# Seven half-size products in place of eight, in the query and output projections of a memory attention on one Trainium2 core

## What is computed

```python
def memory_cross_attention(h, mem_n, wq, wk, wv, wo):
    b, s, _ = h.shape                       # 1, 512
    q = (h @ wq).reshape(b, s, 4, 256)      # wq, wk, wv, wo: 1024 x 1024
    k = (mem_n @ wk).reshape(b, m, 4, 256)  # m = 256
    v = (mem_n @ wv).reshape(b, m, 4, 256)
    logits = jnp.einsum('bqhd,bkhd->bhqk', q, k) * 256 ** -0.5
    probs = jax.nn.softmax(logits, axis=-1)
    out = jnp.einsum('bhqk,bkhd->bqhd', probs, v).reshape(b, s, 1024)
    return out @ wo

# in each of the two layers of the first block
x = x + hybrid_mixer(...)
x = x + memory_cross_attention(rms_norm(x, ...), rms_norm(mem, ...), wq, wk, wv, wo)
```

## Time and profile before

| what | us |
|---|---|
| median of 3 runs | 3501.32 (3500.64 to 3505.17) |
| the profiled execution, its own time | 3494.63 |
| its span, first to last instruction | 3492.8 |
| TensorE busy | 3323.3 (95%) |
| VectorE busy | 1050.0 (30%) |
| ScalarE busy | 973.1 (28%) |
| GpSimd busy | 220.8 (6%) |

### The profile page before, as it was taken

How to read it: one execution, slowest core, us unless ns; L and a number is a source line. 1 busy time by engine, 2 the same in 40 slices (tenths; PEclk the granted TensorE clock), 3 DMA queues, 4 the chain that set the end, 5 groups by cost and what they waited for, 6 DMA issues and landing times.

```text
span 3492.8 us, 44840 instructions
## 1 busy us (share of the span) xinstructions
PE 3323.3 (95%) x18622; PEld 1854.0 (53%) x18622; DVE 1050.0 (30%) x2365; ACT 973.1 (28%) x2062; POOL 220.8 (6%) x256
## 2 busy tenths in 40 slices
PE   8999999999999999999999999979998999997999
PEld 4464454754464454753755777533324756763333
DVE  2224461022224361022352456130002344453011
ACT  1344140111336140123232355031113234442110
POOL 0000000000000000000000055000100000340000
PEclk9999999999999999999999999989999999998999
DMA  4221362312211282312101000159993111013997
GB/s 156 95 77 51 111 258 78 121 43 66 73 64 59 73 302 72 121 51 98 43 25 37 25 2 32 61 189 362 358 334 146 43 37 43 1 62 144 385 409 307
DMA packets 120263, 437.60 MB, mean 125 GB/s; under 512 B 13168, under 2 KB 15344, under 8 KB 119424
## 3 DMA queue, kind: packets, MB, share of 16 engines
q1 hardware_dynamic: 113040, 407.45, 31.9%
q0 software_dynamic: 7024, 27.30, 2.3%
HBM read 422.08 MB, written 12.62 MB: 124 GB/s over the span
## 4 chain that ended last, share of the span: by engine, by line
PE 88%; DVE 5%; ACT 3%; DMA 3%; issue 1%; SPq 0%; POOL 0%; DVEq 0%; ACTq 0%; POOLq 0%
PE bank L1829 85%; DMA ring<-in_stream 1%; PE bank L1944 1%; ACT h_sb L2300 1%; DMA h_sb<-in_stream 1%; PE bank L892 1%; ACT work L2201 0%; DVE work L2369 0%; DVE work L2371 0%; DVE work L1609 0%; DMA work<-in_stream 0%; PE bank L2047 0%; DVE small L1608 0%; DMA work<-tokens,slot_tok 0%; ACT y_sb L2161 0%
## 5 line engine op out<-in xcount | busy, mean ns | idle before, releaser
L1829 PE MATMUL bank<-h_sb,ring 128*128 128x512 f32 (+2 forms) x3200 | 1249.9, 546 | 22.8 <-ACT h_sb L1117 10.8
L1829 PEld LDWEIGHTS bank<-h_sb,ring 128*128 128x128 f32 (+1 forms) x3200 | 590.9, 190 | 579.4 <-issue 535.4
L1829 PE MATMUL bank<-y_sb,ring 128*128 128x512 f32 (+1 forms) x1152 | 471.1, 569 | 3.3 <-DVEq L226 3.3
L1829 PEld LDWEIGHTS bank<-y_sb,ring 128*128 128x128 f32 x1152 | 217.9, 190 | 249.8 <-issue 242.7
L2161 ACT ACTIVATE work<-bank 128x512 f32<-128x512 f32 (+1 forms) x256 | 129.7, 516 | 747.7 <-PE bank L1829 655.2
L1829 PE MATMUL bank<-ring,h_sb 128*128 128x128 f32 (+2 forms) x2144 | 286.4, 313 | 1.4 <-ACT work L1280 0.7
L1829 PEld LDWEIGHTS bank<-ring,h_sb 128*128 128x128 f32 (+2 forms) x2144 | 232.4, 186 | 43.9 <-issue 40.7
L1829 PE MATMUL bank<-work 128*64 128x128 f32 (+7 forms) x1712 | 230.2, 342 | 16.7 <-ACT work L2201 4.2
L1829 PE MATMUL bank<-ring,work 128*64 128x512 f32 (+2 forms) x920 | 225.5, 563 | 2.8 <-DMA ring<-in_stream 2.7
L1829 PEld LDWEIGHTS bank<-work 128*64 128x64 f32 (+2 forms) x1712 | 139.0, 160 | 88.5 <-issue 54.1
L1829 PE MATMUL bank<-y_sb,work 128*64 128x128 f32 (+2 forms) x920 | 170.8, 438 | 1.0 <-DMA y_sb<-in_stream 0.4
(11 more groups left out here) (300 smaller groups left out, 3326.6 us busy)
## 6 DMA issues: line engine op xcount, KB each, us to landing
ring<-in_stream SPq DMA_DIRECT2D x578, 512.0 KB, 4.7
y_sb<-in_stream SPq DMA_DIRECT2D x110, 512.0 KB, 8.1
h_sb<-in_stream SPq DMA_DIRECT2D x40, 512.0 KB, 14.8
work<-in_stream SPq DMA_DIRECT2D x20, 512.0 KB, 15.4
work<-in_bias SPq DMA_DIRECT2D x2, 2688.0 KB, 10.0
tokens<-work POOLq DMA_DIRECT2D x10, 512.0 KB, 4.1
work<-forget POOLq DMA_DIRECT2D x2, 1536.0 KB, 7.0
x_sb<-in_xT SPq DMA_DIRECT2D x4, 512.0 KB, 6.2
```

The source lines that it names most:

```text
L1829: return nc.tensor.matmul(o, a, b, start=first, stop=last, skip_group_check=True)
```

## The change

The first two units of each projection stay as they were. The other six are taken as three pairs. The product of a pair (256 output features, 1024 input features, 512 tokens) is cut in halves each way and made with Strassen's scheme (in Winograd's form): seven products of half size, each four `mm` calls of 256 tokens, in place of eight. The sums of the weight quarters (four of 128 x 512 a pair) are made by GpSimd, one of them in place in the ring; the sums of the input's quarters (four of 128 x 1024 a projection) by VectorE; the results are put together by VectorE from the banks, with one copy by ScalarE a pair. Two sets of buffers for the weight sums are taken in turn (`w_sums[n % 2]`), so the third pair's sums wait until TensorE has started the second pair. The weight sums of the query projection lie in `prob` and `probT`, those of the output projection in the upper half of `h_sb`, which is read until the query projection has ended (`sums_room`).

```diff
@@ -131,6 +131,9 @@
         one_hot_read = sem("one_hot_read")
+        sums_room = sem("sums_room")
+        weight_sums = sem("weight_sums")
+        first_copied = sem("first_copied")
         spread_read = sem("spread_read")
@@ -297,6 +300,21 @@
+        HALF, PAIRS, MEM_SCALE = T // 2, KT // 2, (D_MODEL // 4) ** -0.5
+        FIRST, SECOND = slice(0, HALF), slice(HALF, T)
+        t_sums = [tiles(8192 + 1024 * n, 4, HALF) for n in range(4)]
+        sums_of = lambda v: [v[:, m * 512:(m + 1) * 512] for m in range(3)]
+        query_w_sums = [sums_of(prob), sums_of(probT)]
+        out_w_sums = [sums_of(h_sb[:, 4 * ALL:6 * ALL]), sums_of(h_sb[:, 6 * ALL:8 * ALL])]
+        first_products = [levels_sb[:, n * HALF:(n + 1) * HALF] for n in range(2)]
+        second_sums, fourth_sums = levels_sb[:, T:T + HALF], levels_sb[:, T + HALF:2 * T]
+        mem_ends = [sum(UNITS[p] for _, m, p in ORDER[:ORDER.index((1, l, "mem")) + 1]) for l in range(DEPTH)]
+        def weight_quarters(u):
+            a, b = room(places[u][0]), room(places[u + 1][0])
+            return a[:, 0:512], a[:, 512:1024], b[:, 0:512], b[:, 512:1024]
@@ -1739,6 +1757,21 @@
                 V.dma_start(forget_rows[1], everywhere(forget[2:8, :], 6)).then_inc(forget_in[1], 16)
+                for room_made, first, w_sums in ((memory_read, mem_ends[l] - 2 * KT, query_w_sums),
+                                                 (sums_room, mem_ends[l] - KT, out_w_sums)):
+                    pool.wait_ge(room_made, l + 1)
+                    for n in range(1, PAIRS):
+                        u = first + 2 * n
+                        a11, a12, a21, a22 = weight_quarters(u)
+                        s2, s3, s4 = w_sums[n % 2]
+                        if n == 3:
+                            pool.wait_ge(w_turn, u - 4 + 3)
+                        for slot, use, _ in places[u:u + 2]:
+                            pool.wait_ge(w_loaded[slot], 16 * use)
+                        me.link(V.tensor_tensor(s3, a11, a21, ALU.subtract), weight_sums)
+                        me.link(V.tensor_tensor(a21, a21, a22, ALU.add), weight_sums)
+                        me.link(V.tensor_tensor(s2, a21, a11, ALU.subtract), weight_sums)
+                        me.link(V.tensor_tensor(s4, a12, s2, ALU.subtract), weight_sums)
@@ -1862,6 +1895,29 @@
                 ins.then_inc(full_sem[reader], 1)
+            def seven_products(n, tile, w_sums, reader):
+                a11, a12, a21, a22 = weight_quarters(unit[0])
+                s2, s3, s4 = w_sums
+                t1, t2, t3, t4 = t_sums
+                weights()
+                weights()
+                for m in range(4):
+                    pe.wait_ge(weight_sums, me.nth(weight_sums))
+                if n == 1:
+                    pe.wait_ge(operand_ready, me.nth(operand_ready))
+                for b, read_by, a, of, opens in (
+                        (0, "act", a11, lambda k: tile(k, FIRST), True), (1, "dve", s2, lambda k: t2[:, k, :], True),
+                        (2, "dve", a21, lambda k: t1[:, k, :], True), (3, "dve", s3, lambda k: t3[:, k, :], True),
+                        (0, reader, a12, lambda k: tile(4 + k, FIRST), False),
+                        (2, "dve", s4, lambda k: tile(4 + k, SECOND), False), (3, "dve", a22, lambda k: t4[:, k, :], False)):
+                    claim(b, read_by)
+                    for k in range(4):
+                        ins = mm(banks[b][:, 0:HALF], a[:, k * P:(k + 1) * P], of(k), opens and k == 0, k == 3)
+                        if k == 0 and (a is a11 or a is s4):
+                            ins.then_inc(w_turn, 1)
+                    ins.then_inc(full_sem[read_by], 1)
@@ -2133,13 +2189,19 @@
                     project_tokens(n % 4, lambda k, j: h[:, k, T + j * P:T + (j + 1) * P], 2)
-                for n in range(KT):
+                for n in range(2):
                     project(n % 4, hk, T, fresh=n == 0)
+                for n in range(1, PAIRS):
+                    seven_products(n, lambda k, of: h[:, k, of], query_w_sums[n % 2], "act")
                 all_read("act")
+                all_read("dve")
+                me.notify(sums_room)
                 attention(mem_units(), scores_in, turned)
                 pe.wait_ge(operand_ready, me.nth(operand_ready))
-                for n in range(KT):
+                for n in range(2):
                     project(n % 4, lambda k: y[:, k, :], T, "dve")
+                for n in range(1, PAIRS):
+                    seven_products(n, lambda k, of: y[:, k, of], out_w_sums[n % 2], "dve")
@@ -2212,6 +2274,12 @@
                     project_out(n)
+            def first_copy(n, **kw):
+                bank_full()
+                me.link(A(first_products[n % 2], banks[0][:, 0:HALF], ACT.Copy, **kw), freed_by_act)
+                me.notify(first_copied)
@@ -2320,9 +2388,14 @@
                              banks[n % 4][:, 0:MEM].rearrange("p (j n) -> p j n", j=2))
-                for n in range(8):
-                    evacuate(flat(n * T, T), banks[n % 4][:, :], scale=(D_MODEL // 4) ** -0.5)
+                for n in range(2):
+                    evacuate(flat(n * T, T), banks[n % 4][:, :], scale=MEM_SCALE)
+                for n in range(1, PAIRS):
+                    first_copy(n, scale=MEM_SCALE)
+                    evacuate(flat(2 * n * T, HALF), banks[0][:, 0:HALF], scale=MEM_SCALE)
                 attention(mem_units(), scores_in, turned)
+                for n in range(1, PAIRS):
+                    first_copy(n)
@@ -2570,10 +2643,50 @@
                 norm(h[:, :, 0:T], x[:, :, 0:T], lambda k: par1(l, A_XQ + k), slice(0, T))
+                def input_sums(v):
+                    t1, t2, t3, t4 = t_sums
+                    low, high = v[:, 0:4, :], v[:, 4:8, :]
+                    me.link(V.tensor_tensor(t1, low[:, :, SECOND], low[:, :, FIRST], ALU.subtract))
+                    me.link(V.tensor_tensor(t2, high[:, :, SECOND], t1, ALU.subtract))
+                    me.link(V.tensor_tensor(t3, high[:, :, SECOND], low[:, :, SECOND], ALU.subtract), wait=False)
+                    me.link(V.tensor_tensor(t4, high[:, :, FIRST], t2, ALU.subtract), operand_ready)
+                def scaled_into(o, i, b, scale):
+                    bank_full()
+                    me.link(V.scalar_tensor_tensor(out=o, in0=banks[b][:, 0:HALF], scalar=scale, in1=i, op0=ALU.mult,
+                                                   op1=ALU.add), freed_by_dve)
+                input_sums(h[:, :, 0:T])
+                q = tiles(0, 8, T)
+                for n in range(1, PAIRS):
+                    a, b = 2 * n, 2 * n + 1
+                    await_(first_copied)
+                    scaled_into(second_sums, first_products[n % 2], 1, MEM_SCALE)
+                    scaled_into(fourth_sums, second_sums, 2, MEM_SCALE)
+                    scaled_into(q[:, b, SECOND], fourth_sums, 3, MEM_SCALE)
+                    scaled_into(q[:, a, SECOND], second_sums, 2, MEM_SCALE)
+                    scaled_into(q[:, b, FIRST], second_sums, 3, MEM_SCALE)
                 attention(mem_units(), scores_in)
                 me.notify(operand_ready)
-                for n in range(KT):
+                input_sums(y[:, 0:8, :])
+                for n in range(2):
                     added(n)
+                into = lambda o, i, s=None: me.link(V.tensor_tensor(o, o, i, ALU.add), s)
+                for n in range(1, PAIRS):
+                    a, b = 2 * n, 2 * n + 1
+                    await_(first_copied)
+                    scaled_into(second_sums, first_products[n % 2], 1, 1.0)
+                    scaled_into(fourth_sums, second_sums, 2, 1.0)
+                    into(x[:, a, SECOND], second_sums)
+                    into(x[:, b, FIRST], second_sums)
+                    into(x[:, b, SECOND], fourth_sums)
+                    for v, bank in ((x[:, b, SECOND], 3), (x[:, a, FIRST], 0), (x[:, a, SECOND], 2), (x[:, b, FIRST], 3)):
+                        bank_full()
+                        into(v, banks[bank][:, 0:HALF], freed_by_dve)
+                    me.notify(act_input)
```

## The result

The changed kernel takes 3478.5 us (median of 6 runs, 3473.6 to 3487.1), the kernel before 3501.0 in the same comparison: a ratio of 0.9941 with a 95% interval of 0.9928 to 0.9954, so 16 to 25 us less. 3486.1 was predicted, in a range of 3478 to 3495: the median lies 7.6 us under the forecast and half a microsecond inside the range. The profiled execution took 3478.32 us, 16.3 less than that of before, where 15.2 had been forecast.

A forecast was written before the change was run, and what follows sets the result against it. TensorE, holding 88% of the chain, was taken to bound the kernel. Matmul time -19.8, ends -0.8 and blocking beside the attention +5.4 gave -15.2 us: 3486.1 against the median of 3501.3, range 3478 to 3495.

The forecast's parts named there:

- rival without blocking: At the attention's start, GpSimd and VectorE don't get in each other's way: the 5.4 us fall away, 3480.7; chance 0.16.
- TensorE's time: Query and output projections: 168 half-width instructions replace 96 full ones, 4.9 us less a projection, 19.8 over four.
- The ends: Last query result and last output addition leave by shorter VectorE steps: together 0.8 us less over both layers.
- Bank claims: Inside a pair, products 5, 6 and 7 reuse banks already read, with two products (3.46 us) between: cost nothing.
- input sums: VectorE's four sums of 128 x 1024 a projection, 4.9 us, are ready before they are wanted: cost nothing.
- weight sums: GpSimd's four sums a pair, 1.45 us each, 5.8 us; the third pair allows up to 3.0 a step: cost nothing.
- turns: In a pair's second unit `w_turn` rises at 8.7 us, not 6.9, so one load in two starts 1.8 us later: nothing.
- GpSimd's queue: The sums stand behind the decay table's transfers and ahead of the next layer's and the second block's memset: nothing.
- GpSimd beside the attention: At the attention's start, output weight sums block VectorE's scalings of units one and two: 2.7 us a layer, 5.4 in all.
- Shut out until the eighth sum is done: At the attention's start, GpSimd keeps VectorE's scalings waiting through all eight sums: only 6.0 us gained, 3495.3; chance 0.10.
- Late sums: The third pair's GpSimd sums take 4 us a step, TensorE waits 16 us in all: 3502.1, no change; chance 0.05.
- late banks: TensorE waits for VectorE's bank readings at four of seven products, 28 us in all: slower, 3514; chance 0.04.

The follow-up runs named there:

- sums_after: The changed kernel with `sums_room` raised behind TensorE's attention, so GpSimd's output weight sums start only then: 0.9939 of the kernel before (0.9915 to 0.9963).

## Why the prediction was right

The mechanism held, term by term, with one price too high. The total alone would not show that. The median, 3478.5, lies nearer to the rival without blocking (3480.7) than to the forecast, and it is inside the range only by the 3 us that the lower end was given for where a median falls; so much of it is luck. The stretches decide between the two, since the blocking is in the trace.

**TensorE's time.** 4.9 us a projection, 19.8 in all, from 0.4305 and 0.2166 us an instruction. The output stretches lost 5.2 and 5.1 us and the query stretches, without the cost of `sums_room`, 5.0 (55.79 to 50.80), ends included. Right.

**The ends.** The output end was to bring 0.28 us a layer and fits (5.2 of 4.9 + 0.3). The query end was to bring 0.13 and cost 0.1 to 0.2 (the stretch lost 4.7 and 4.8 us of the 4.9 of the matmuls): the `notify` ahead of the attention was not priced. It is 0.15 to 0.24 us a layer.

**What was costed at nothing.** Bank claims (no gap, and the limit found between two and three times the work), input sums (4.9 us, over at 654.7), weight sums (1.34 us a step, forecast 1.45, limit 3.0), turns and GpSimd's queue: all held. VectorE's combining steps took 0.42 us, not 0.48. In a query pair ScalarE makes two steps of 0.38 us and not the one copy of the section on the change: it also scales the result of bank 0 into SBUF. It sat idle for 4.8 us or more before each of the later ones, so this costs nothing.

**GpSimd beside the attention: right in kind, three times too large.** The forecast was 2.7 us a layer, measured 0.9 to 1.0. A scaling with one input in SBUF is blocked: that was the open question, and the rival without it is ruled out by the 1.85 and 2.33 us. The loss in a pair of scalings was put at 2.15 us; it was 1.24 for the first unit, whose first scaling began near the end of a sum, and 1.72 for the second. And 0.8 us of slack was taken off before the next maxima as if everything left went through: TensorE's scores of unit two came 3.27 us after unit one's and those of unit three 3.53 after that, where they were 3.31 and 3.19 before, and the rest, 0.6 us, comes ahead of the second unit's last transposes, where the profile marks 0.36 us of idle time. "SBUF — State Buffer" of the Trainium skill (the two sides of SBUF) has VectorE steps with two SBUF inputs, or in a two-port mode, under an exclusive lock with GpSimd's. The traces agree: two scalings took 0.61 us alone and 1.85 to 2.35 beside GpSimd, sums on two SBUF inputs 1.23 and 2.17, GpSimd's own 1.26 and 2.13, and steps that read a bank were unchanged. That the scalings run in such a mode is not shown. For it speaks that one of 256 columns took 0.31 us alone where a step of the same width that reads a bank took 0.42. But a scaling also reads a 128 x 1 factor from SBUF, and no run separates the two.

**The rivals.** Shut out until the eighth sum is done: no, the scalings ended at 724.24 and 728.26, GpSimd at 729.46. Late sums, late banks: no, with the distances above. The sum was -15.2 us; the stretches gave -18.1, and behind the difference of 2.9 stands the block's price (5.4 forecast, 1.9 measured), less 0.6 for what the query's end cost in place of its gain.

## What to carry to other kernels

Where TensorE's chain is unbroken and the others are idle, one product in eight can be bought with sums on the idle engines; the pace of the half-size instructions is to be read from the trace first. Ask of each new GpSimd step which VectorE steps it meets, and what stands behind these in VectorE's queue: the same eight sums cost 0.9 us at the attention's start, 1.2 in its middle and nothing right behind it. A plain part that is kept as a cover should be checked for whether the cover is needed: ahead of the queries it was not, and 1.7 us a layer lay there.

## What the runs showed of the hardware that I had not expected

A VectorE step with a single wide SBUF input can be held by a GpSimd step as one with two is: two scalings of 128 x 256, each with a 128 x 1 factor, took 1.85 to 2.35 us instead of 0.62, while a step on one bank and one SBUF buffer stayed at 0.42 us beside such sums (697.51 in the changed kernel, with a sum from 697.17). It goes both ways: GpSimd's step of 128 x 512 took 2.13 us instead of 1.26 beside VectorE's 1024-wide sums. And a semaphore raised by TensorE without a matmul, where TensorE's next start waits behind it, cost 0.15 to 0.24 us; in `sums_after` it reached GpSimd while matmuls that stand before it were still to run.
